# The last third of a second block's modulation vector: row products on GpSimd and row sums on ScalarE instead of matmuls

## What is computed

```python
sc = jax.nn.silu(c)
for l in range(2):
    shift, scale, gate = jnp.split(sc @ w_ada[l] + b_ada[l], 3, axis=-1)        # w_ada: [2, 2048, 6144]
    shift_c, scale_c, gate_c = jnp.split(scc @ w_ada[l] + b_ada[l], 3, axis=-1) # the same for the context
    h = rms(x, norm_w[l]) * (1.0 + scale) + shift
    ...                                                  # projections, three kinds of attention
    x = x + gate * merge_out(o_a, o_b, o_c, z, w_out[l])
    if l == 0:
        xc = xc + gate_c * merge_out(...)                # the context is only updated in layer 0
```

## Time and profile before

| what | value |
|---|---|
| time, median of 3 runs | 3334.0 us (3332.7 to 3334.08) |
| the profiled execution | 3330.97 us, span 3329.2 us |
| TensorE busy | 3292.0 us, 99% of the span |
| chain that ended last, by engine | PE 92%, DVE 3%, ACT 2% |
| mods, L2074, over the whole program | 3% of the chain |
| stretch of `out0` | about 2470 to 2654 us of the span |

### The profile page before, as it was taken

One profiled execution on the slowest core, in us unless ns is written; L12 is line 12 of the kernel. 1 busy time (PEld: TensorE's weight loads), 2 busy tenths in 40 slices (PEclk: granted clock), 3 DMA queues, 4 the chain that ended last, 5 costly groups with the idle time before them and its releaser, 6 DMA issues.

```text
span 3329.2 us, 56166 instructions
## 1 busy us (share of the span) xinstructions
PE 3292.0 (99%) x20496; PEld 2783.3 (84%) x20496; DVE 2153.0 (65%) x3219; ACT 1413.2 (42%) x2160; POOL 589.1 (18%) x531
## 2 busy tenths in 40 slices
PE   8999999999999999999999999999999999999999
PEld 8999999989987777778887787778877788888978
DVE  7887877567776667777764566634553475774665
ACT  5444445544434343454532423532342263544353
POOL 4999920111540000000300000000001100000000
PEclk9999999999999999999999999999999999999999
DMA  6555555565777777777722222121236443422225
GB/s 221 182 181 183 185 185 186 185 209 167 244 272 266 282 259 275 266 259 269 247 101 96 73 89 76 51 83 64 94 108 208 140 152 108 138 91 95 95 97 181
DMA packets 158862, 554.51 MB, mean 167 GB/s; under 512 B 17456, under 2 KB 23728, under 8 KB 158640
## 3 DMA queue, kind: packets, MB, share of 16 engines
q1 hardware_dynamic: 154144, 534.67, 47.3%
q0 software_dynamic: 4496, 16.78, 1.5%
HBM read 545.09 MB, written 6.29 MB: 166 GB/s over the span
## 4 chain that ended last, share of the span: by engine, by line
PE 92%; DVE 3%; ACT 2%; DVEq 1%; issue 1%; ACTq 1%; DMA 0%; POOL 0%; SPq 0%
PE psum L2020 17%; PE psum L2022 17%; PE psum L2021 17%; PE psum L2045 14%; PE psum L2046 7%; PE psum L2225 4%; PE psum L2074 3%; PE psum L2371 2%; PE psum L2397 2%; PE psum L2226 2%; PE psum L2382 2%; PE psum L2146 1%; DVE wlo L1253 1%; PE psum L2328 1%; ACTq L869 0%
## 5 line engine op out<-in xcount | busy, mean ns | idle before, releaser
L1253 DVE TENSOR_TENSOR wlo<-raw,whi 128x1024 fp32r<-128x1024 f32 (+3 forms) x844 | 1030.6, 1226 | 533.8 <-ACT whi L798 504.7
L798 ACT ACTIVATE whi<-raw 128x1024 fp32r<-128x1024 f32 (+3 forms) x844 | 864.5, 1029 | 1047.3 <-PE psum L2022 605.6
L2020 PE MATMUL psum<-hcat,whi 128*128 128x256 f32 (+1 forms) x3436 | 1133.5, 330 | 5.2 <-DVE wlo L1253 4.6
L2022 PE MATMUL psum<-hcat,wlo 128*128 128x256 f32 (+1 forms) x3436 | 1109.7, 323 | 0.0
L2021 PE MATMUL psum<-hcat,whi 128*128 128x256 f32 (+1 forms) x3436 | 1109.4, 323 | 0.0
L2020 PEld LDWEIGHTS psum<-hcat,whi 128*128 128x128 f32 x3436 | 653.1, 190 | 90.5 <-issue 34.7
L2045 PE MATMUL psum<-hcat,whi 128*128 128x512 f32 x2048 | 727.2, 399 | 0.1
L2021 PEld LDWEIGHTS psum<-hcat,whi 128*128 128x128 f32 x3436 | 653.6, 190 | 52.0 <-issue 3.8
L2022 PEld LDWEIGHTS psum<-hcat,wlo 128*128 128x128 f32 x3436 | 653.1, 190 | 51.6
L2046 PE MATMUL psum<-hcat,wlo 128*128 128x256 f32 x2048 | 572.9, 280 | 0.0
L2045 PEld LDWEIGHTS psum<-hcat,whi 128*128 128x128 f32 x2048 | 384.6, 188 | 115.1 <-issue 25.6
(11 more groups left out here) (266 smaller groups left out, 3406.2 us busy)
## 6 DMA issues: line engine op xcount, KB each, us to landing
raw<-in_stream SPq DMA_DIRECT2D x978, 512.0 KB, 4.2
raw<-in_stream SPq DMA_DIRECT2D x18, 384.0 KB, 3.0
raw<-in_stream SPq DMA_DIRECT2D x24, 256.0 KB, 2.6
resid_dram<-X POOLq DMA_DIRECT2D x2, 2048.0 KB, 8.7
bias<-in_natten POOLq DMA_DIRECT2D x16, 256.0 KB, 2.9
X<-resid_dram POOLq DMA_DIRECT2D x4, 1024.0 KB, 6.1
raw<-in_stream SPq DMA_DIRECT2D x16, 192.0 KB, 2.6
X<-in_xT SPq DMA_DIRECT2D x4, 512.0 KB, 7.2
```

What stands on the lines that cost most here:

```text
L798: act.activation(whi[:, c % HI_SLOTS, 0:n], raw[:, slot, 0:n], ACT.Copy).then_inc(hi_ready, 1)
L1253: vec.tensor_tensor(wlo[:, slot, 0:n], raw[:, slot, 0:n], whi[:, c % HI_SLOTS, 0:n].bitcast(F32), ALU.subtract).then_inc(lo_ready, 1)
L2020: pe.matmul(dst, h, cat[:, kk, c0:c0 + width], start=(q == 0 and k == 0), stop=False)
L2022: last = pe.matmul(dst, l_, cat[:, kk, c0:c0 + width], start=False, stop=(q == nq - 1 and k == nch - 1))
```

## The change

The 32 quarters of the last third of layer 1's `w_ada` are laid out anew on the host: a quarter now holds, for 128 outputs (one to a partition), half of the 2048 inputs along the row. GpSimd multiplies a quarter with the same half of `silu(c)`, which lies as a row in every partition (`crow`), into one of two buffers `row_product`; ScalarE sums each product along its row by a copy with an accumulator. `silu(c)` gets into that form by way of DRAM: GpSimd stores it early and loads it as a broadcast ahead of `out0`. TensorE has no matmul, transpose or wait for mods left, but it is TensorE that frees the slots: before the last matmul of a tile it waits for the products of that turn and then raises `weights_used` for the second quarter and all mods of the turn at once. VectorE loses `mod_add` and `mod_rows` in `out0` and adds halves and bias at the start of `out1`. The mods lie 2, 2, 3, 2, 2, 3, ... to a turn, in turns 1 to 14.

```diff
-MOD_OUT = [0] + [4] * 4 + [2] * 8 + [0] * 3
+MOD_OUT = [0] + [2, 2, 3, 2, 2, 3, 2, 2, 3, 2, 2, 3, 2, 2] + [0]
@@ ScalarE, out0
                 for t, e in enumerate(OUT_WEAVE):
-                    for k in range(2 if t < KD - 1 else 1):
-                        hi(C0["out0"] + 2 * t + k + AHEAD)
+                    hi(C0["out0"] + 2 * t + AHEAD)
+                    for _, a in e["mods"]:
+                        act.wait_ge(gate_mods, a + 1)
+                        act.activation(row_product[:, a % 2, :], row_product[:, a % 2, :], ACT.Copy,
+                                       accum_out=gate_half[:, a // 2, a % 2:a % 2 + 1]).then_inc(row_summed, 1)
+                    if t < KD - 1:
+                        hi(C0["out0"] + 2 * t + 1 + AHEAD)
                     act.wait_ge(x_tile, XT["out0"] + t + 1)
@@ VectorE
+            vec.tensor_tensor(c_silu[:, :], cvec[:, :, 0], csig[:, :, 0], ALU.mult)
...
                 if l:
+                    vec.wait_ge(row_summed, 2 * KD)
+                    j = 48 + 2 * KD
+                    vec.tensor_tensor(ada_t[:, 0, j:j + KD], gate_half[:, :, 0], gate_half[:, :, 1], ALU.add)
+                    fence()
+                    vec.tensor_tensor(ada_t[:, 0, j:j + KD], ada_t[:, 0, j:j + KD], pv("b_ada", j, KD), ALU.add)
+                    fence()
                     out_tiles(0)
...
-                        mod_add(e, OUT_BLOCK)
-                        mod_rows(e, s, 0)
@@ TensorE, tile (out_chunks the same)
+                        if rows and q == nq - 1 and k == nch - 1:
+                            pe.wait_ge(gate_mods, rows[-1][1] + 1)
                         last = pe.matmul(dst, l_, cat[:, kk, c0:c0 + width], start=False,
                                          stop=(q == nq - 1 and k == nch - 1))
                         if k == nch - 1:
-                            last.then_inc(weights_used, 1)
+                            last.then_inc(weights_used, 1 + (len(rows) if q == nq - 1 else 0))
@@ TensorE, out0
-                    mod_fold(e, OUT_BLOCK)
-                    mod_quarters(e["mods"], Q0["out0"], 0)
@@ GpSimd
+            pool.wait_ge(vector_stage, STAGE["silu_c"])
+            pool.dma_start(c_dram.rearrange("(p k) -> p k", p=P), c_silu[:, :]).then_inc(c_stored, 16)
             for c in range(FF_REST):
...
+                if l == 0:
+                    pool.wait_ge(c_stored, 16)
+                    pool.wait_ge(vt_used, VTS_OF["c0"][-1] + 1)
+                    pool.dma_start(crow[:, :], c_dram.unsqueeze(0).to_broadcast([P, P * KD])).then_inc(crow_in, 16)
...
                     pool.memset(racc[:, 0, :], 0.0)
                     pool.drain()
+                    pool.wait_ge(crow_in, 16)
                     for k in range(KD - 1):
+                        for pos, a in OUT_WEAVE[k]["mods"]:
+                            s = Q0["out0"] + pos
+                            pool.wait_ge(raw_in[s % SLOTS], 16 * (s // SLOTS + 1))
+                            if a >= 2:
+                                pool.wait_ge(row_summed, a - 1)
+                            pool.tensor_tensor(row_product[:, a % 2, :], raw[:, s % SLOTS, :], crow[:, QW * (a % 2):QW * (a % 2) + QW],
+                                               ALU.mult).then_inc(gate_mods, 1)
                         add_square(RS["out0"] + k, k % 2, 0, racc[:, 0, :])
```

More of the change, by code:

```diff
@@ L273, in build @@
     region("work", 16 * KIB)
+    region("gate_mod", 3 * KD * 4)
     raw = sb("raw", [SLOTS, QW], F32, "raw")
@@ L314, in build @@
     hfull = sb("hfull", [2, 2, S], F32, "q", 28 * KIB)
+    crow = sb("crow", [2 * QW], F32, "q", 0)
+    row_product = sb("row_product", [2, QW], F32, "q", 8 * KIB)
+    c_silu = sb("c_silu", [KD], F32, "gate_mod", 0)
+    gate_half = sb("gate_half", [KD, 2], F32, "gate_mod", KD * 4)
     ln_sum = sb("ln_sum", [2, S], F32, "q", 20 * KIB)
@@ L395, in build @@
         c_sig = sem("c_sig")
+        c_stored = sem("c_stored")
+        crow_in = sem("crow_in")
+        gate_mods = sem("gate_mods")
+        row_summed = sem("row_summed")
         rows_ready = sem("rows_ready")
@@ L2006, in weight, with tile @@
                 return whi[:, c % HI_SLOTS, col:col + n], wlo[:, SQ[c] % SLOTS, col:col + n]
-            def tile(s, d, ts, td, cat, c0, loff, width, nq=2, nch=8, k0=0, ready=None, beside_=None):
+            def tile(s, d, ts, td, cat, c0, loff, width, nq=2, nch=8, k0=0, ready=None, beside_=None, rows=()):
                 pe.wait_ge(psum_free, FREE[ts] + td)
@@ L2442, in last_out0, with out_chunks @@
                 return last
-            def out_chunks(l, t, a, b):
+            def out_chunks(l, t, a, b, rows=()):
                 s, ts, w = C0[f"out{l}"] + 2 * t, T0[f"out{l}"] + t, chunks_w(l)
@@ L2454, in out_chunks @@
                         pe.wait_ge(ycat_lo, len(YCAT) * l + sum(first <= kk for first, _ in YCAT))
+                    if rows and kk == KD - 1:
+                        pe.wait_ge(gate_mods, rows[-1][1] + 1)
                     h, l_ = weight(s + kk // 8, P * (kk % 8))
@@ L2465, in out_chunks @@
                     if kk % 8 == 7:
-                        last.then_inc(weights_used, 1)
+                        last.then_inc(weights_used, 1 + (len(rows) if kk == KD - 1 else 0))
             for l in range(LAYERS):
@@ L2525, in _ @@
                     if t < 2:
-                        out_chunks(l, t, Y_EARLY, KD)
+                        out_chunks(l, t, Y_EARLY, KD, rows=e["mods"])
                     elif t < KD - 1:
-                        tile(C0["out0"] + e["cpos"], 0, T0["out0"] + t, 0, hcat, 0, 2 * S, w, k0=Y_PLACE)
+                        tile(C0["out0"] + e["cpos"], 0, T0["out0"] + t, 0, hcat, 0, 2 * S, w, k0=Y_PLACE,
+                             rows=e["mods"])
                     else:
                         last_out0(0).then_inc(half_done, 1)
-                    mod_fold(e, OUT_BLOCK)
-                    mod_quarters(e["mods"], Q0["out0"], 0)
         @block.gpsimd
@@ L2704, in _stream @@
     ada = w["w_ada_2"].reshape(LAYERS, 8, 2, P, 12, 512).transpose(0, 4, 1, 3, 2, 5).reshape(-1, P, QW)
+    rows = w["w_ada_2"][1][:, 2 * D:].reshape(KD, P, KD, P).transpose(2, 3, 1, 0).reshape(KD, P, 2, QW)
+    ada = np.concatenate([ada[:8 * OUT_BLOCK], rows.transpose(0, 2, 1, 3).reshape(-1, P, QW)])
     def put_woven(weave_, tiles_, mod0):
```

1 line of the change is left out of this document (added).

## The result

The changed kernel takes **3382.3 us** (median of four runs, 3381.31 to 3384.86) against 3333.6 for the kernel before on the same chip: a ratio of 1.015, with a 95% interval of 1.0138 to 1.0161, 49 us slower. The profiled execution took 3381.48 us with a span of 3379.7; before it was 3330.97.

What follows compares the result with a forecast made beforehand. TensorE was taken to bound the kernel, busy 161.58 of 161.80 us from tile 2 to 14 of `out0`. Terms: -19.0 + 12.4 + 9.4 + 32 + 10.3 + 7 + 2 = +54, so 3388 us; forecast 3368 to 3408, range 3356 to 3408.

Steps and rivals of the forecast that it cites:

- loads: In eight turns of `out0`, ScalarE's `hi` waits for a quarter freed only at tile end: 4.0 us each, +32.
- the ring: Products, sums, `hi`, `lo`, additions, square, GpSimd's addition, next products: 11.95 us against a 10.99 tile, 13 turns, +12.4.
- contention: GpSimd's products and VectorE's `lo` slow each other on the shared port: 0.52 us in 14 turns, +7, bounds 0 and 17.
- marks given for the profile after: Signs if right: first wait near 10 us, then threes of about 1, 7 and 5; full waits 70 us in sum.
- the clock: TensorE at half speed after waits, behind tile 1 and the second wait of each three: +2 us, bounds 0 and 10.
- The work removed: Mod matmuls and transposes leave TensorE in `out0`, all on the path: -19.0 us.
- The third products: The four turns of `out0` with a third product take 2.36 us more each: +9.4.
- The first wait: Tile 1's last matmul waits for turn 1's products, which stand behind GpSimd's drain and first addition: +10.3 us, bounds 8 and 12.
- The end of `out0`: Square and addition of the last tile come the same time after it as before: costed at nothing.
- TensorE's share of the stretch: TensorE's busy share from tile 2 to tile 14 of `out0`, claimed to fall from 99.9% to some 75%.
- the one without load waits: Rival: slower, but all quarters are in when asked for, so without the 32: 3356 us, chance 10%.
- the average is right: Rival: products under 1.8 us fit in a tile and loads land in time: 3324 or 3315 us, chance 5%.

Runs made afterwards that it cites:

- a_none: The changed kernel without GpSimd's products, ScalarE's row sums and the waits for them, quarters still loaded: 3311.8 us, ratio 0.9936 to the kernel before.
- a_mod4: The changed kernel with mods dealt 2 to a turn in turns 1 to 12 and 4 in turns 13 and 14: 3369.8 us, ratio 1.0106.
- a_hoist: The changed kernel with the products of turn 1 put ahead of GpSimd's clearing of `racc` and drain: 3377.3 us, ratio 1.0133.
- a_release: The changed kernel, second quarter freed by its tile's last matmul without waiting, mods waited for and freed at the next tile's first matmul: 3363.3 us, ratio 1.0091.
- a_three: The changed kernel with turn 1's products ahead of the drain, turn t+1's ahead of turn t's addition, and a third product buffer: 3319.1 us, ratio 0.9957.
- a_ctx: The changed kernel with the last of GpSimd's four DMAs, the second half of the context, issued by ScalarE: 3381.8 us, ratio 1.0148.
- a_ahead: The changed kernel with GpSimd doing the products of turn k+1, not k, ahead of the addition of turn k: 3338.2 us, ratio 1.0014.
- a_half: The changed kernel with products and row sums over 512 of each mod's 1024 columns: 3353.6 us, ratio 1.0055.

## Why the prediction was right

The forecast was 3388 us; measured 3382. The working holds in its parts too, with small errors of both signs: loads 4 and the ring 2 too high, contention 3.4 too low. That contention takes back over half of the other two, so that the total comes nearer than its parts, is luck. Some of the marks given for the profile after were off, as said below under the clock.

**The work removed**, 19.0 us. `a_none` is 21.4 us under the kernel before by medians (interval 16 to 27), and tile 15 starts 19.7 us earlier. With a tile of 10.88 us the removal comes to about 1.4 more and the ring's waits to as much more, which leaves the sum as it is.

**The ring**, predicted 11.95 us without contention. In `a_mod4` it is 12.59 with it. Its parts: 5.62 us idle for sum, `hi`, `lo`, additions and square, 1.29 the addition, 0.24 the hand-over, 5.44 two products. Two products alone take 4.64 in turn 1. So the ring without contention is 11.79, which makes 13 x (11.79 - 10.99) = 10.4 us, predicted 12.4. The product was the only price not in the trace of before: 2.32 us measured where the slope of two widths gave 2.36.

**Contention**, predicted 7. It is 5.44 - 4.64 = 0.80 us a turn, 13 x 0.80 = 10.4. VectorE's timeline of the kernel after explains the 0.80:

```profile
2499.99 1.48 DVE L1269 TENSOR_TENSOR wlo<-raw,whi 128x1024 fp32r<-128x1024 f32 x1 [1.79 <-ACT whi L809]
```

This `wlo` ends at 2501.47, and the product that starts at 2500.63 is 0.81 longer than a free one, the 0.84 us until that end. The rule of the Trainium skill (SBUF — State Buffer, "SBUF: two separate sides"), an exclusive lock held for a whole instruction, agrees with that. My reading of it, a whole `lo` of 1.22 a turn, was too much: the later one pays only what is left of the first. The same stands in all 13 turns: the first product takes 3.04 to 3.10 us beside the last 0.8 of a `wlo`, the others 2.34 to 2.40. `a_hoist` shows contention where it is dear, a `wlo` 5.2 us late behind two products; there the rule does not fit as it stands, for by its record the `wlo` began 0.6 us before the first of them.

**The third products**, predicted 9.4. They add 7.65 - 5.45 = 2.2 us each in the first turn of three, about 9 in four.

**The loads**, predicted 4.0 in eight turns, 32. There are eight waits of ScalarE for loads, 27.9 us, and a turn of two with one takes 16.2 on the mean against 12.6 without: 3.6 more (3.5 in the turns of three), 28 in all. `a_mod4` and `a_release` show that it is the count of positions and the late release.

**The first wait**, predicted 10.3, is 10.5.

**The clock**, predicted 2. The windows of the kernel after, in the first wait, behind it and after that:

```profile
2487.60:2493.50 5.90, 0.00 (x0) 0.00 (x0) 0.00 (x0) 1.15 (x2) 5.70 (x3) 0.50 0.00 0
2493.50:2497.50 4.00, 3.97 (x9) 3.17 (x10) 1.79 (x3) 2.09 (x3) 0.00 (x0) 0.50 0.30 84
2498.00:2502.00 4.00, 4.00 (x19) 3.29 (x18) 1.69 (x2) 1.68 (x3) 2.67 (x2) 1.00 0.79 260
```

Half speed for some 4 us behind the wait costs 2. But the ring is late by 1.6 us in the next turn anyway, and TensorE then does not wait in it: about 0.4 us are left. The same in turns 5, 8 and 14. This is why the short wait of "about 1" was seen only in turn 11 (1.4 us). Term: 0 to 1.

The clock did more than this term says, and two marks missed it. The waits were to be 70 us in sum and are 51.8; those of "5" are 3.9, 3.3, 2.5 and 2.1. What is missing is TensorE at half clock, busy where the forecast had it idle. Tiles 2 to 14 of `a_none` and of the kernel after (columns as above):

```profile
2484.21:2625.65 141.44, 141.44 (x625) 117.16 (x624) 52.82 (x67) 36.97 (x53) 18.09 (x14) 1.00 0.62 213
2494.97:2695.10 200.13, 158.84 (x625) 127.02 (x624) 51.59 (x65) 68.45 (x111) 96.22 (x43) 0.89 0.43 147
```

The same matmuls take 17.4 us more. Nearly all of it costs nothing here, because the ring sets the pace and the slow matmuls only fill what would have been waiting: 51.8 + 17.4 = 69 is what the ring, the loads and the first wait take together.

**The end of `out0`**, costed at nothing, is 1.5 us longer from the start of tile 15 to z1, with a wait of 1.3 for GpSimd's last additions.

Sum: -19.0 + 10.4 + 10.4 + 9 + 28 + 10.5 + 0.5 = +49.8. The profiled executions differ by 50.5, the medians by 48.7. The end of `out0` would bring the sum to 51.3. TensorE's share of the stretch was forecast at some 75% and is 76%, but that is luck: the forecast's own sum, 145 busy of 216 us, gives 67%, and the share is higher because of the 17 us at half clock.

Of the **rivals**, the one without load waits falls by `a_mod4` and `a_release`; "the average is right" would have needed a product under 1.8 us. Its number, 3315, is nearly what `a_three` reaches (3319) with products of 2.86: the average was not wrong about the engines' capacity, it was wrong about the order that the change gives them.

## What to carry to other kernels

Before work is moved to an idle engine, follow one item round all engines, with its hand-overs: if the moved step waits for a result that itself waits for the moved step's last turn, the length of that circle is what counts, and here it was 12.6 us in a tile of 11.0 while no engine was over half full, TensorE aside. Then break the circle and buffer it: one turn ahead gave back 44 of 49 us, the first turn ahead of a drain and a third buffer the rest and more. Count the ring of load slots too, for a slot that is freed half a turn late cost 3.5 us here in each of the eight turns that needed it.

## What the runs showed of the hardware

- GpSimd's drain behind DMAs that it issued itself ends 0.6 us after the last of these has landed (0.58 to 0.63 in the profiles of both kernels and of all ten experiments), though its record is 12.0 to 13.2 us long. In `a_hoist` the instruction before it ended 4.8 us later and the drain at nearly the same time, and in `a_ctx` it ended a microsecond before another engine's DMA landed.
- A VectorE instruction of 1.23 us beside two back-to-back products of GpSimd took 6.45 us: it did not get in between them. The record of it begins at 2475.3, 0.6 us before the first product, while GpSimd was issuing a DMA. Issuing the DMA is not enough to hold it: in the changed kernel the same `wlo` starts at 2475.2 beside the same issue and takes 1.22. Why it lost to products that began after it is open.
- With products running beside nearly every conversion (`a_three`), `wlo` takes 2.03 us in place of 1.23 and a product 2.86 in place of 2.32.
- The granted clock of TensorE did not follow the length of a short wait: behind 1.93 and 2.37 us it fell to 0.50 for some 3 us (`a_ahead`), behind 2.40 (`a_ahead`), 2.51 (the changed kernel) and 3.47 (`a_half`) it stayed at 1.00. In or behind the waits of 3.9 to 13.2 us it stood at 0.50 each time. Half clock is lost only where nothing else is later: in `a_ahead` TensorE's 5.5 us of longer busy time add to its waits, in the changed kernel nearly all of 17.4 us is hidden by the ring.
